# Two encoder layers on one core: one shift row on TensorE, sines in the opening, splits ahead of head roots, late rows in VectorE's gap, column sums asked for one unit on

## The chip, the cores and the metric

One core of one Trainium2 chip. The metric is the device time of one execution in microseconds (us), the median of three runs.

## What is computed

Two layers work on x of 1024 tokens by 1024 channels. Layer 0 has sliding-window attention with per-head sinks, query and key norms and rotary positions; layer 1 has a gated MLP whose gate is mixed along the sequence by a triangular 128x128 matrix per channel group. A squared-ReLU MLP of width 4096 follows each. Ahead of every sub-layer stands an RMS norm whose gain and shift come from the conditioning vector c.

```python
cond = jax.nn.silu(c)
for i in range(DEPTH):                                   # DEPTH = 2
    mod = (cond @ mod_w[i] + mod_b[i])[:, None, :]
    shift1, scale1, gate1, shift2, scale2, gate2 = jnp.split(mod, 6, axis=-1)
    h = rms_norm(x, norm1_gain[i]) * (1 + scale1) + shift1
    y = swa_sink_attention(...) if i == 0 else gmlp_spatial_gating(...)
    x = x + gate1 * y
    h = rms_norm(x, norm2_gain[i]) * (1 + scale2) + shift2
    x = x + gate2 * squared_relu_mlp(h, mlp_w1[i], mlp_w2[i])
```

## The kernel before

Activations lie transposed in SBUF: eight chunks of 128 channels by 1024 tokens. Every float32 product with a weight is made of three matmuls, since both sides are split into a high part (fp32r) and the rest: `w_hi` by `h_hi`, `w_hi` by `h_lo`, `w_lo` by `h_hi`. A **unit** is one output chunk of 128 channels: eight steps k over the input chunks, six 512-column matmuls each (L1463), 48 in all. Where only half of the tokens is done, it is 24. Units go in pairs over two weight slots. For each, SyncE loads `w_raw`, ScalarE writes `w_hi` (`split_hi`, L493), GpSimd or VectorE writes `w_lo` (`split_lo`, `first_low`), and TensorE waits in `ready` (L1452) for `lo_done` and for its PSUM tile to be emptied (`evac`). A hook is a piece of other TensorE work set behind a step k of a unit. The engines' orders are written out by hand and joined by semaphores.

The modulation `cond @ mod_w` is made on VectorE: it adds 128x1024 rows, scaled by an element of `cond`, into an accumulator (one instruction a row, eight rows a part), TensorE transposes the accumulator (`mod_columns`, L1550), and VectorE sums the columns and adds the bias (`first_part`, `mod_part`). Places that matter here:

- **The opening.** SyncE loads x, 16 rows `mod_first` (eight of scale1, then eight of shift1) and two weight blocks. VectorE works out the angles of the rotary positions, then adds the scale rows into `mod_acc` and those shift rows into `qa` that TensorE does not take as small matmuls (L1615, `ROWS_BY_TENSOR`, 3 rows). The squares of x go over `ss_done`, a root on ScalarE, `ss_mm`, a reciprocal and a spread copy on VectorE, and transposes (`spread_norm`, L1583) to PSUM. Then h is made chunk by chunk: `scaled` (VectorE), `h_hi` (ScalarE, L517), `low` (VectorE, L1095). `normed_pair` (L1478) multiplies as chunks come.
- **The queries.** Pair 0 is the keys and the first half of a query pair. Four steps j follow. For each, ScalarE empties PSUM and squares (`first_half`, L580), VectorE adds the squares (L1187), TensorE sums them by head (`head_squares`, a hook, L1564), ScalarE takes roots and spreads reciprocals (`head_roots`), TensorE transposes them (`head_spread`, L1571), and VectorE rotates (`turn`), norms, and adds modulation rows between (`mods`, L896).
- **The closing of attention** (`closing`): the output projection in two halves of the tokens. Behind it VectorE adds the residual, sums squares, splits weights (L954), makes h, and adds 16 **late rows** (L967) by the counts of `LATE_ROWS`: the rows of parts 4 and 5 of the modulation, which `mod_columns(4)` and `mod_columns(5)` transpose.
- **The opening of the MLP** (`opening_pair`, L1521): the first pair of up-units, first on the first token half, then on the second as its h comes. `mod_columns(5)` follows it (L1548).
- **The gated MLP** (L1385 to L1446): `bn_stats` over v, then `mod_part(11)`, the aggregate, a memset of the mixing tile `ws`, loads of `ws` and `bias` by ScalarE's queue, and `blend` (L1827), the mixing matmuls of TensorE, hooked at k = 4 of the second u-unit.

Of the kernel before, what the change touches and what calls it, by code (L numbers as in the profile page):

```python
# [14 lines left out]
P = 128  # L15
# [19 lines left out]
ROWS_BY_TENSOR = 3  # L35
# [30 lines left out]
LATE_ROWS = ((0, 0, 1, 2, 1, 2, 2), (0, 0, 1, 0, 1, 1, 2, 0, 3))  # L66
# [7 lines left out]
def build(nc, x_in, c_in, pos_in, weights, mod_w, cols, mats, ws_in, bias_in, q_dram, v_dram, out):  # L74
# [5 lines left out]
    with ctx:  # L80
# [96 lines left out]
        first_used, row_cols = sem("first_used"), sem("row_cols")  # L177
# [310 lines left out]
        def _(act):  # L488
# [64 lines left out]
            for k in range(KC):  # L553
                if k % 2 == 0:
                    act.wait_ge(x_ld[k // 2], 16)
                nc.scalar.activation(square_tile(k), x[:, k, :], ACT.Square).then_inc(sq_done, 1)
            act.wait_ge(const_in, 48)
            nc.scalar.activation(root[:, 0:1], eps, ACT.Sqrt)
            act.wait_ge(ss_done, KC)
            for half in range(2):  # L560
                nc.scalar.activation(tmp[0:1, 1, columns_of(half)], pp[0][0:1, columns_of(half)], ACT.Sqrt,
                                     bias=eps[0:1, :], scale=1.0 / D).then_inc(sd_done, 1)
            split_hi(0, 0)
# [16 lines left out]
            def first_half(j):  # L580
# [5 lines left out]
                split_hi(j + 1, 1)  # L586
                act.wait_ge(evac[1], j + 1)
# [13 lines left out]
            act.wait_ge(angle, 1)  # L601
            nc.scalar.activation(cos[:, :], cos[:, :], ACT.Sin).then_inc(trig, 1)
            nc.scalar.activation(sin[:, :], sin[:, :], ACT.Sin).then_inc(trig, 1)
# [3 lines left out]
            first_half(0)  # L607


            for j in range(4):  # L610
# [17 lines left out]
                if j < 3:  # L628
                    load_mod(4 * j + 6, 0)
                    load_mod(4 * j + 7, 1)  # L630
                    first_half(j + 1)
# [252 lines left out]
        def _(dve):  # L884
# [21 lines left out]
            def mod_part(part, tile=None):  # L906

                dve.wait_ge(mod_mm, part + 1)
                V.memset(mod_acc[:, :], 0.0).then_inc(acc_zero, 1)
                dve.wait_ge(acc_zero, part)  # L910
# [21 lines left out]
            def closing(pair0, n, gate, late=False, first=None):  # L932
# [88 lines left out]
                split_lo(KC - 1)  # L1021
                dve.wait_ge(bc_done, 2 * n + 2)
# [8 lines left out]
                if late:  # L1031
                    late_rows(LATE_ROWS[1][KC])
                    mod_part(5, pp[2])
# [68 lines left out]
            first_row(KC + ROWS_BY_TENSOR, KC)  # L1102
# [4 lines left out]
            first_row(KC + ROWS_BY_TENSOR + 1, KC + 1)  # L1107
            first_row(KC + ROWS_BY_TENSOR + 2, KC + 2)
            for half in range(2):
                dve.wait_ge(ss_mm, half + 1)  # L1110
                own(V.reciprocal(inv[:, 4 * half:4 * half + 4], pp[2][:, HALF * half:HALF * half + 4]))
                V.tensor_copy(mod_t[:, 0, columns_of(half)].rearrange("p (b m) -> p b m", m=P),
# [811 lines left out]
```

## Time and profile before

| | us |
|---|---|
| median of 3 runs | 2365.39 |
| lowest, highest | 2364.77, 2367.08 |
| the profiled execution, its own time | 2365.93 |
| its span | 2364.1 |
| TensorE busy / VectorE / ScalarE / GpSimd | 2301.6 / 1256.7 / 693.6 / 759.9 |

The profile is one execution. Its rows give a start in us from the start of the span, a duration, and in brackets how long the engine stood idle ahead of the row and what ended that. 1.83 us of that execution's time lie outside its span.

### The profile page before, as it was taken

What the parts mean: (1) busy time and instruction counts of PE and PEld (TensorE: products, weight loads), DVE (VectorE), ACT (ScalarE), POOL (GpSimd) and SP (SyncE); (2) the same over time, 40 slices, a digit from 0 to 9 for tenths busy, and PEclk for the clock granted to TensorE, in tenths of its full rate; (3) what the DMA queues carried; (4) which work ended last, traced back from release to release, by engine and by line L of the source; (5) the groups of instructions that cost most, each with busy time, mean ns of one, the idle gap of its engine ahead of it and who ended that gap; (6) DMA issues with size and microseconds to landing.
All of it is one profiled execution on the core that took longest, in us unless ns stands there. A gap on an engine that the chain in (4) does not pass through costs nothing.

```text
span 2364.1 us, 29197 instructions
## 1 busy us (share of the span) xinstructions
PE 2301.6 (97%) x10332; PEld 1837.8 (78%) x10332; DVE 1256.7 (53%) x1562; ACT 693.6 (29%) x940; POOL 759.9 (32%) x566
## 2 busy tenths in 40 slices
PE   7898998999999999999999999999999999999999
PEld 5786676888888888777887888877788888888887
DVE  6677678565565564564334431456655455555321
ACT  3325533232232232233222210223323223322220
POOL 0123420544544452311221212122154455355221
PEclk7999999999999999999999999999999999999999
DMA  6353332122112212223333221122111111111112
GB/s 253 98 160 97 144 144 80 54 81 94 60 69 89 71 62 98 89 89 107 123 121 137 80 79 51 65 80 89 54 49 51 54 53 44 44 62 44 54 45 89
DMA packets 82119, 201.33 MB, mean 85 GB/s; under 512 B 23809, under 2 KB 29825, under 8 KB 81538
## 3 DMA queue, kind: packets, MB, share of 16 engines
q1 hardware_dynamic: 63650, 139.70, 17.6%
q10 hardware_dynamic: 18400, 60.69, 7.2%
q8 instruction: 45, 0.74, 0.1%
q14 instruction: 24, 0.20, 0.0%
HBM read 182.54 MB, written 16.78 MB: 84 GB/s over the span
## 4 chain that ended last, share of the span: by engine, by line
PE 83%; issue 12%; POOL 2%; DVE 2%; ACT 1%; DMA 0%; DVEq 0%; POOLq 0%; ACTq 0%; SPq 0%
PE pp L1463 61%; PE pp L1768 20%; PE pp L1832 1%; POOL pr L428 1%; POOL w_lo L414 1%; PE pp L1806 1%; DVE mod_t L947 1%; DVE h_lo L982 0%; PE pp L1557 0%; DMA w_raw<-weights 0%; PE pp L1578 0%; DVE mod_acc L896 0%; ACT w_hi L493 0%; ACT tmp L526 0%; PE pp L1587 0%
## 5 line engine op out<-in xcount | busy, mean ns | idle before, releaser
L414 POOL TENSOR_TENSOR w_lo<-w_raw,w_hi 128x1024 fp32r<-128x1024 f32 x144 | 349.3, 2426 | 1301.3 <-ACT w_hi L493 1301.3
L1463 PE MATMUL pp<-h_hi,w_hi 128*128 128x512 f32 x1824 | 603.7, 402 | 22.3 <-DVE h_lo L982 6.9
L1463 PE MATMUL pp<-h_lo,w_hi 128*128 128x512 f32 x1824 | 595.4, 397 | 0.0
L1463 PE MATMUL pp<-h_hi,w_lo 128*128 128x512 f32 x1824 | 595.1, 397 | 0.0
L1463 PEld LDWEIGHTS pp<-h_hi,w_hi 128*128 128x128 f32 x1824 | 341.0, 189 | 112.4 <-DVE h_lo L982 15.0
L1463 PEld LDWEIGHTS pp<-h_hi,w_lo 128*128 128x128 f32 x1824 | 344.7, 189 | 83.4
L1463 PEld LDWEIGHTS pp<-h_lo,w_hi 128*128 128x128 f32 x1824 | 344.8, 189 | 81.8
L1330 DVE SCALAR_TENSOR_TENSOR x<-pp,mod,x 128x512 f32<-128x512 f32 x336 | 252.1, 750 | 242.1 <-PE pp L1768 242.1
L493 ACT ACTIVATE w_hi<-w_raw 128x1024 fp32r<-128x1024 f32 x170 | 179.7, 1057 | 634.9 <-PE pp L1463 511.8
L1768 PE MATMUL pp<-c_lo,w_hi 128*128 128x512 f32 x672 | 265.8, 396 | 0.0
L1768 PE MATMUL pp<-c_hi,w_hi 128*128 128x512 f32 x672 | 265.8, 396 | 0.0
L1768 PE MATMUL pp<-c_hi,w_lo 128*128 128x512 f32 x672 | 265.8, 396 | 0.0
L1463 PE MATMUL pp<-hid_hi,w_hi 128*128 128x512 f32 x512 | 182.7, 397 | 3.0 <-DVE hid_lo L1430 2.2
L1463 PE MATMUL pp<-hid_hi,w_lo 128*128 128x512 f32 x512 | 181.9, 395 | 0.0
L1463 PE MATMUL pp<-hid_lo,w_hi 128*128 128x512 f32 x512 | 181.9, 395 | 0.0
L455 POOL TENSOR_TENSOR w_lo<-s_w,w_hi 128x768 fp32r<-128x768 f32 x96 | 122.8, 1297 | 117.8 <-ACT w_hi L704 117.8
L1768 PEld LDWEIGHTS pp<-c_lo,w_hi 128*128 128x128 f32 x672 | 126.3, 188 | 30.6
L1768 PEld LDWEIGHTS pp<-c_hi,w_hi 128*128 128x128 f32 x672 | 126.3, 188 | 30.5
L1768 PEld LDWEIGHTS pp<-c_hi,w_lo 128*128 128x128 f32 x672 | 126.3, 188 | 30.4
L1278 DVE SCALAR_TENSOR_TENSOR c_f<-pp,tmp 128x512 f32<-128x512 f32 x72 | 47.5, 687 | 180.3 <-ACT tmp L711 180.3
L455 POOL TENSOR_TENSOR w_lo<-w_raw,w_hi 128x256 fp32r<-128x256 f32 x96 | 97.5, 1016 | 104.9 <-ACT w_hi L704 102.1
L704 ACT ACTIVATE w_hi<-s_w 128x768 fp32r<-128x768 f32 x96 | 60.8, 634 | 209.1 <-PE pp L1768 155.9
(182 smaller groups left out, 2284.4 us busy)
## 6 DMA issues: line engine op xcount, KB each, us to landing
w_raw<-weights SPq DMA_DIRECT2D x218, 512.0 KB, 3.5
mod_t<-mod_w ACTq DMA_DIRECT2D x64, 512.0 KB, 4.0
mod_first<-mod_w SPq DMA_DIRECT2D x16, 512.0 KB, 15.4
mod_late<-mod_w ACTq DMA_DIRECT2D x2, 4096.0 KB, 22.8
v_dram<-v_out ACTq DMA_DIRECT2D x16, 512.0 KB, 5.3
vf<-v_dram ACTq DMA_DIRECT2D x16, 512.0 KB, 3.3
x<-x_in SPq DMA_DIRECT2D x4, 1024.0 KB, 8.1
qf<-q_dram SPq DMA_DIRECT2D x32, 128.0 KB, 2.2
```

The costliest lines, as they stand in the source:

```text
L414: nc.gpsimd.tensor_tensor(out=w_lo[:, s, :, :], in0=w_raw[:, s, :, :], in1=w_hi[:, s, :, :].bitcast(f32), op=ALU.subtract).then_inc(lo_don ...
L428: nc.gpsimd.tensor_tensor(out=pr[:, b, :, 0:P], in0=pr[:, b, :, 0:P], in1=small[:, b, 3, :].unsqueeze(2).to_broadcast([P, 4, P]), op=ALU.m ...
L455: nc.gpsimd.tensor_tensor(out=down_target(w_lo, part), in0=down_source(part, q), in1=down_target(w_hi, part).bitcast(f32), op=ALU.subtract ...
L493: nc.scalar.activation(w_hi[:, s, :, :], w_raw[:, s, :, :], ACT.Copy).then_inc(hi_done, 1)
L704: nc.scalar.activation(down_target(w_hi, part), down_source(part, q), ACT.Copy).then_inc(d_hi, 1)
L947: V.tensor_tensor(out=sumsq[:, columns_of(half)], in0=sumsq[:, columns_of(half)], in1=tmp[:, s, columns_of(half)], op=ALU.add).then_inc(ss ...
L1278: V.scalar_tensor_tensor(out=out, in0=src[:, columns_of(half)], scalar=0.0, in1=tmp[:, s, columns_of(half)], op0=ALU.max, op1=ALU.mult).th ...
L1330: V.scalar_tensor_tensor(out=xn, in0=banks[BANK[t]], scalar=mod[:, 6 * layer + GATE2, 2 * q + m:2 * q + m + 1], in1=xn, op0=ALU.mult, op1= ...
L1463: last = T.matmul((pp[s] if tile is None else tile)[:, cs], w[:, s, k, :], r[:, k, cs], start=(k == 0 and w is w_hi and r is hi), stop=(k ...
L1768: last = T.matmul(banks[BANK[t]], w[:, slot, k, :], r[:, i, OPERAND[t], :], start=(t in FRESH and i == 0 and w is w_hi and r is c_hi), sto ...
L1806: last = T.transpose(pp[2][:, P * b:P * b + P], tmp[:, s, P * b:P * b + P], ident[:, :])
L1832: last = T.matmul(pp[2][:, P * b:P * b + P], vf[:, s, b, :], ws[:, bass.ds(i, 1), :].rearrange("p a t -> p (a t)"), start=True, stop=True)
```

## The change

In the opening, ScalarE makes the sines ahead of the first root, and writes the spread copies that VectorE wrote; TensorE makes the token sums ahead of `mod_columns(0)`, and takes one shift row where it took three; VectorE takes seven and is put in another order. In the queries, `first_half` is cut in `first_copy` (copy and `split_hi`) and `first_square`, and the first `first_copy` stands ahead of `head_roots(0)`; two rows of `mods` go behind the addition of squares of j = 0. In the closing, `mod_columns(4)` is hooked one unit later and the token sums two steps later; one late row goes from the end to u = 7, and the last two ahead of the second half's h. `mod_columns(5)` goes ahead of the second half of the opening pair, into another PSUM tile, with a wait on `mod_done` behind the pair. In the gated MLP `mod_part(11)` goes behind the first two `normalised`, without its memset, and the first blend is hooked at k = 7.

```diff
-ROWS_BY_TENSOR = 3
+ROWS_BY_TENSOR = 1
-LATE_ROWS = ((0, 0, 1, 2, 1, 2, 2), (0, 0, 1, 0, 1, 1, 2, 0, 3))
+LATE_ROWS = ((0, 0, 1, 2, 1, 2, 2), (0, 0, 1, 0, 1, 1, 2, 1, 2))
...
+            act.wait_ge(angle, 1)
+            nc.scalar.activation(cos[:, :], cos[:, :], ACT.Sin).then_inc(trig, 1)
+            nc.scalar.activation(sin[:, :], sin[:, :], ACT.Sin).then_inc(trig, 1)
             act.wait_ge(const_in, 48)
...
+            for half in range(2):
+                act.wait_ge(inv_done, half + 1)
+                nc.scalar.activation(mod_t[:, 0, columns_of(half)].rearrange("p (b m) -> p b m", m=P),
+                                     inv[:, 4 * half:4 * half + 4].unsqueeze(2).to_broadcast([P, 4, P]),
+                                     ACT.Copy).then_inc(rb_done, 1)
...
-            act.wait_ge(angle, 1)
-            nc.scalar.activation(cos[:, :], cos[:, :], ACT.Sin).then_inc(trig, 1)
-            nc.scalar.activation(sin[:, :], sin[:, :], ACT.Sin).then_inc(trig, 1)
+            first_copy(0)
             head_roots(0, KV)
             load_mod(2, 0)
             load_mod(3, 1)
-            first_half(0)
+            first_square(0)
...
-            def mod_part(part, tile=None):
+            def mod_part(part, tile=None, last=False):
...
                 split_lo(KC - 1)
+                if late:
+                    late_rows(LATE_ROWS[1][KC])
                 dve.wait_ge(bc_done, 2 * n + 2)
...
                 if late:
-                    late_rows(LATE_ROWS[1][KC])
-                    mod_part(5, pp[2])
+                    mod_part(5, pp[1])
...
             dve.wait_ge(q_bc, 1)
             V.tensor_tensor(out=oa[:, 0, :], in0=oa[:, 0, :], in1=pp[2][:, :], op=ALU.mult).then_inc(k_roped, 2)
-            mods(2)
...
                 V.tensor_tensor(out=tmp[:, 0, :], in0=tmp[:, 0, :], in1=tmp[:, 1, :], op=ALU.add).then_inc(q_sum, 1)
+                if j == 0:
+                    mods(2)
...
-                mod_part(10 + half)
+                if half == 0:
+                    mod_part(10)
...
             dve.wait_ge(v_sc, 1)
+            dve.wait_ge(mod_mm, PARTS)
             V.memset(ws[64:128, :, 0:64], 0.0).then_inc(wsz, 1)
...
-                with dve.Fori(0, 3) as i:
+                if kb == 0:
+                    normalised(1, 1, 1)
+                    mod_part(PARTS - 1, last=True)
+                    gated(0, 0, more=False)
+                    gated(0, 1)
+                with dve.Fori(0 if kb else 1, 3) as i:
...
-                    unit(pair0 + 3, 1, hi, lo, halves=(0,), hooks={5: columns})
+                    unit(pair0 + 3, 1, hi, lo, halves=(0,))
...
-                unit(pair0 + 4, 0, hi, lo, halves=(1,), hooks={4: lambda: token_squares(n, 0)})
+                hooks = {1: columns, 6: lambda: token_squares(n, 0)} if columns else {4: lambda: token_squares(n, 0)}
+                unit(pair0 + 4, 0, hi, lo, halves=(1,), hooks=hooks)
...
+                if n == 1:
+                    pe.wait_ge(evac[1], pair)
+                    mod_columns(5, mf_used, 2 * KC, tile=pp[1])
                 for k in range(KC + LAG):
...
-                if n == 1:
-                    mod_columns(5, mf_used, 2 * KC, tile=pp[2])
...
-            mod_columns(0, first_used, KC)
...
                 last.then_inc(ss_mm, 1)
+            mod_columns(0, first_used, KC)
...
                 opening_pair(pair0, 2 * layer + 1, (pp[3], pp[0]))
+                if layer == 0:
+                    pe.wait_ge(mod_done, 6)
...
-                unit(kb * KC + U_GU // 2, 1, h_hi, h_lo, hooks={4: lambda: blend(kb * KC, 0, kb, 0)})
+                unit(kb * KC + U_GU // 2, 1, h_hi, h_lo, hooks={4 if kb else 7: lambda: blend(kb * KC, 0, kb, 0)})
```

VectorE in the opening, behind the eight scale rows, before. `qa` takes the shift rows, `inv` and `mod_t` are the norm's reciprocals and their spread, the two `col_sum` are parts 1 and 0 of the modulation, and `shift_b` waits for TensorE's rows:

```order
18 L1069 TENSOR_SCALAR qa<-mod_first,cond 128x1024
19 L1076 TENSOR_REDUCE col_sum<-pp 128x8
20 L1079 TENSOR_TENSOR mod<-col_sum,colt 128x8
21 L1105 SCALAR_TENSOR_TENSOR amp<-mod,colt 128x8
22 L1071 SCALAR_TENSOR_TENSOR qa<-mod_first,cond,qa 128x1024 x2
23 L1111 RECIPROCAL inv<-pp 128x4
24 L1112 COPY mod_t<-inv 128x512
25 L1111 RECIPROCAL inv<-pp 128x4
26 L1112 COPY mod_t<-inv 128x512
27 L1071 SCALAR_TENSOR_TENSOR qa<-mod_first,cond,qa 128x1024
28 L1116 TENSOR_TENSOR shift_b<-pp,colt 128x8
29 L1071 SCALAR_TENSOR_TENSOR qa<-mod_first,cond,qa 128x1024
```

The same place after:

```order
18 L1080 TENSOR_SCALAR qa<-mod_first,cond 128x1024
19 L1082 SCALAR_TENSOR_TENSOR qa<-mod_first,cond,qa 128x1024
20 L1118 RECIPROCAL inv<-pp 128x4 x2
21 L1082 SCALAR_TENSOR_TENSOR qa<-mod_first,cond,qa 128x1024 x2
22 L1087 TENSOR_REDUCE col_sum<-pp 128x8
23 L1090 TENSOR_TENSOR mod<-col_sum,colt 128x8
24 L1123 SCALAR_TENSOR_TENSOR amp<-mod,colt 128x8
25 L1082 SCALAR_TENSOR_TENSOR qa<-mod_first,cond,qa 128x1024 x2
26 L1128 TENSOR_TENSOR shift_b<-pp,colt 128x8
27 L1082 SCALAR_TENSOR_TENSOR qa<-mod_first,cond,qa 128x1024
```

Seven shift rows stand where five stood, six of them ahead of `shift_b` where there were four, and the two copies are gone from VectorE.

ScalarE ahead of the queries' loop, before (`root` and `tmp<-inv` are the head roots of the keys, `qa<-pp` the first copy of the queries, `w_hi<-w_raw` behind it the split for the next slot):

```order
26 L602 ACT_TABLE_LOAD
27 L602 ACTIVATE cos<-cos 128x1024
28 L603 ACTIVATE sin<-sin 128x1024
29 L570 ACT_TABLE_LOAD
30 L570 ACTIVATE root<-pp,colt 128x16
31 L575 ACTIVATE tmp<-inv 128x8x64 x2
32 L499 DMA mod_t<-mod_w 128x1024 x2
33 L585 ACTIVATE qa<-pp 128x1024
34 L493 ACTIVATE w_hi<-w_raw 128x1024
35 L588 ACTIVATE tmp<-qa 128x1024
```

and after:

```order
30 L593 ACTIVATE qa<-pp 128x1024
31 L493 ACTIVATE w_hi<-w_raw 128x1024
32 L578 ACTIVATE root<-pp,colt 128x16
33 L583 ACTIVATE tmp<-inv 128x8x64 x2
34 L499 DMA mod_t<-mod_w 128x1024 x2
35 L598 ACTIVATE tmp<-qa 128x1024
```

The split now waits for nothing but its weights and the end of pair 0; the sines and both table loads are gone from here.

## Rows read from the trace of the kernel before

**Rows 1.** The page, part 1: busy time, share of the span, instructions

```profile
PE 2301.6 (97%) x10332; PEld 1837.8 (78%) x10332; DVE 1256.7 (53%) x1562; ACT 693.6 (29%) x940; POOL 759.9 (32%) x566
```

**Rows 2.** TensorE's waits: who waited for whom, us in total, times, longest

```profile
PE pp L1557 <- DVE mod_acc L896: 2.5, 1, 2.5
```

**Rows 3.** The timeline of TensorE in the opening: start, us, instruction, idle before it

```profile
33.98 10.40 PE L1615 MATMUL pp<-cond,mod_first 128*128 128x1 f32 x48
...
52.57 1.19 PE L1463 MATMUL pp<-h_hi,w_hi 128*128 128x512 f32 x2 [4.64 <-DVE h_lo L1095]
```

**Rows 4.** The timeline of VectorE in the opening

```profile
18.90 9.63 DVE L1071 SCALAR_TENSOR_TENSOR mod_acc<-mod_first,cond,mod_acc 128x1024 f32<-128x1024 f32 x7
30.87 0.75 DVE L1069 TENSOR_SCALAR qa<-mod_first,cond 128x1024 f32<-128x1024 f32 x1 [2.34 <-DMA mod_first<-mod_w]
...
44.42 0.17 DVE L1116 TENSOR_TENSOR shift_b<-pp,colt 128x8 f32<-128x8 f32 x1 [6.26 <-PE pp L1615]
...
49.40 0.17 DVE L1079 TENSOR_TENSOR mod<-col_sum,shift_b 128x8 f32<-128x8 f32 x1
```

**Rows 5.** The timeline of TensorE in the queries

```profile
96.21 1.22 PE L1463 MATMUL pp<-h_hi,w_hi 128*128 128x512 f32 x2 [3.37 <-POOL w_lo L414]
...
100.55 1.04 PE L1571 MATMUL pp<-ident,tmp 128*128 128x128 f32 x8
...
108.65 2.72 PE L1564 MATMUL pp<-colt,tmp 128*128 128x4 f32 x16 [2.87 <-DVE tmp L1187]
111.23 1.20 PE L1463 MATMUL pp<-h_hi,w_hi 128*128 128x512 f32 x2
...
122.07 1.03 PE L1571 MATMUL pp<-ident,tmp 128*128 128x128 f32 x8
...
137.82 1.84 PE L1564 MATMUL pp<-colt,tmp 128*128 128x4 f32 x16
139.52 0.71 PE L1463 MATMUL pp<-h_hi,w_hi 128*128 128x512 f32 x2
...
147.99 1.04 PE L1571 MATMUL pp<-ident,tmp 128*128 128x128 f32 x8
```

**Rows 6.** The timeline of ScalarE in the queries

```profile
119.43 1.02 ACT L585 ACTIVATE qa<-pp 128x1024 f32<-128x1024 f32 x1 [5.58 <-DVE mod_acc L896]
```

**Rows 7.** The timeline of VectorE in the queries

```profile
102.86 4.60 DVE L896 SCALAR_TENSOR_TENSOR mod_acc<-mod_t,cond,mod_acc 128x1024 f32<-128x1024 f32 x2
...
108.52 1.27 DVE L1182 SCALAR_TENSOR_TENSOR oa<-qa,qgain,cos 128x1024 f32<-128x1024 f32 x1
...
116.36 2.66 DVE L896 SCALAR_TENSOR_TENSOR mod_acc<-mod_t,cond,mod_acc 128x1024 f32<-128x1024 f32 x2
```

**Rows 8.** The timeline of TensorE in the closing of attention

```profile
325.72 1.05 PE L1578 MATMUL pp<-ones,mod_t 128*128 128x1 f32 x8 [0.73 <-DVE mod_t L947]
```

**Rows 9.** The timelines at the MLP's opening: VectorE, then GpSimd, then TensorE

```profile
377.89 1.41 DVE L974 SCALAR_TENSOR_TENSOR tmp<-x,amp,pp 128x512 f32<-128x512 f32 x2 [2.89 <-PE pp L1587]
...
396.03 2.64 POOL L414 TENSOR_TENSOR w_lo<-w_raw,w_hi 128x1024 fp32r<-128x1024 f32 x1 [70.92 <-ACT w_hi L493]
...
401.74 1.19 PE L1463 MATMUL pp<-h_hi,w_hi 128*128 128x512 f32 x2 [4.12 <-DVE tmp L1278]
...
406.81 0.62 PE L1463 MATMUL pp<-h_hi,w_hi 128*128 128x512 f32 x2
```

**Rows 10.** The timelines at the first blend: VectorE, then TensorE

```profile
1282.37 0.91 DVE L909 MEMSET mod_acc<- 128x1024 f32 x1 [3.53 <-PE pp L1557]
...
1294.20 2.05 PE L1832 MATMUL pp<-ws,vf 128*128 128x128 f32 x8 [2.31 <-issue]
...
1297.53 0.72 PE L1463 MATMUL pp<-h_hi,w_hi 128*128 128x512 f32 x2
```

**Rows 11.** Windows of TensorE: stretch, length, busy, granted clock, DMA share, GB/s

```profile
319.00:320.00 1.00, 1.00 (x9) 1.00 0.00 0
...
402.00:404.00 2.00, 2.00 (x5) 0.50 0.61 240
```

More of the change, by code:

```diff
@@ L176, in build @@
         pos_s, pos_f, pos_b = sem("pos_s"), sem("pos_f"), sem("pos_b")
-        first_used, row_cols = sem("first_used"), sem("row_cols")
+        first_used, row_cols, inv_done = sem("first_used"), sem("row_cols"), sem("inv_done")
         dv = sem("dv")
@@ L578, in head_roots, with first_copy @@
                 ins.then_inc(q_rb, 1)
-            def first_half(j):
+            def first_copy(j):
                 act.wait_ge(gemm, U_Q + 2 * j + 1)
@@ L586, in first_half, with first_square @@
                 split_hi(j + 1, 1)
+            def first_square(j):
                 act.wait_ge(evac[1], j + 1)
@@ L630, in _ @@
                     load_mod(4 * j + 7, 1)
-                    first_half(j + 1)
+                    first_copy(j + 1)
+                    first_square(j + 1)
             nc.scalar.activation(root[:, 0:1], root[:, 0:1], ACT.Exp)
@@ L904, in mod_step @@
                 scale_add(mod_t[:, slot, :], k, mt_used)
-            def mod_part(part, tile=None):
+            def mod_part(part, tile=None, last=False):
                 dve.wait_ge(mod_mm, part + 1)
-                V.memset(mod_acc[:, :], 0.0).then_inc(acc_zero, 1)
-                dve.wait_ge(acc_zero, part)
+                if not last:
+                    V.memset(mod_acc[:, :], 0.0).then_inc(acc_zero, 1)
+                    dve.wait_ge(acc_zero, part)
                 V.tensor_reduce(out=col_sum[:, :], in_=(pp[3] if tile is None else tile)[:, :].rearrange("p (k c) -> p k c", c=P),
@@ L1101, in _ @@
                 first_row(q, q)
-            first_row(KC + ROWS_BY_TENSOR, KC)
+            rows = [KC + ROWS_BY_TENSOR + i for i in range(KC - ROWS_BY_TENSOR)]
+            first_row(rows[0], KC)
+            first_row(rows[1], KC + 1)
+            for half in range(2):
+                dve.wait_ge(ss_mm, half + 1)
+                V.reciprocal(inv[:, 4 * half:4 * half + 4], pp[2][:, HALF * half:HALF * half + 4]).then_inc(inv_done, 1)
+            first_row(rows[2], KC + 2)
+            first_row(rows[3], KC + 3)
             first_part(1, SCALE1, mod_b(SCALE1))
@@ L1106, in _ @@
                                        op0=ALU.add, op1=ALU.mult))
[L1107 to L1112, printed above, removed]
-                              inv[:, 4 * half:4 * half + 4].unsqueeze(2).to_broadcast([P, 4, P])).then_inc(rb_done, 1)
-            first_row(KC + ROWS_BY_TENSOR + 3, KC + 3)
+            first_row(rows[4], KC + 4)
+            first_row(rows[5], KC + 5)
             dve.wait_ge(row_cols, 1)
             own(V.tensor_tensor(out=shift_b[:, :], in0=pp[1][:, 0:KC], in1=mod_b(SHIFT1), op=ALU.add))
-            first_row(KC + ROWS_BY_TENSOR + 4, KC + 4)
-            first_low(0)
+            first_row(rows[6], KC + 6)
             dve.wait_ge(bc_done, 2)
             scaled(0, 0)
+            scaled(1, 1)
             first_part(2, SHIFT1, shift_b[:, :])
-            scaled(1, 1)
+            first_low(0)
             dve.wait_ge(mod_done, 2)
```

## The prediction

> **What bounds the kernel now.** I read the page's first part before anything else: TensorE is busy for 2301.6 us of 2364.1 [rows 1], so only its idle 62.5 us, and what it does at its lower clock, can be won. The next view is its waits, longest first, and then the timelines around each. Six places matter: the start of the first unit at 52.57 [rows 3], two waits in the queries of 3.37 and 2.87 us [rows 5], 2.5 us for late rows [rows 2], 0.73 us behind it [rows 8], 4.12 us at the opening of the MLP [rows 9] and 2.31 us at the first blend [rows 10]. The change touches all of them and little else.
>
> A wait costs twice where the granted clock falls with it: in windows it reads 0.50, which is 1.2 GHz, or 1.00, which is 2.4 GHz [rows 11]. At full speed the 18 groups of two 512-column matmuls from 139.52 to 147.99 take 8.47 us, 0.47 each; the same 18 from 111.23 to 122.07 take 10.84 [rows 5]. So the clock lost 2.4 us there. After 2.5 us of idle at the late rows the clock still read 1.00 in the window 319:320 [rows 2, 11]; after 2.87 it had fallen.
>
> **The change, part by part.** Times below are of the profiled execution: span 2364.1, its own time 2365.93, 0.5 above the median 2365.39. I subtract from all alike.
>
> *The opening.* TensorE's first unit starts when h of chunk 0 is there, which hangs on part 0 of the modulation, made at 49.40+0.17 = 49.57 [rows 4]. VectorE's chain to it holds 2.34 us idle for a row's DMA and 6.26 idle for TensorE's three rows [rows 4]. These are 48 matmul records in 10.40 us [rows 3], so one row is 16 records, 3.5 us, and its wait goes: TensorE gets to it about when the reciprocals are made. New chain, from the end of the scale rows at 28.53 (18.90+9.63): row 9 at once (0.75); row 10 when it has landed. Row 11 landed at 30.87 and rows come at about 1.27 us (412 GB/s in this stretch, half a MB each, an estimate of mine), so row 10 ends near 30.9; reciprocals 0.4; rows 11 and 12, 2.6; sum, bias and gain of part 1, 1.65; rows 13, 14, 15, 3.8; `shift_b` 0.2; two `scaled` 2.4; reduction and bias 1.4. That ends at 43.4, 6.2 us earlier than 49.57. The moved `first_low` (1.2) lies under ScalarE's `h_hi`. The sines, 2.1 us and a table load, fall in 6.6 us in which ScalarE waited for the sum of squares; were that cover gone, they would cost their 3.4. The spread copies on ScalarE are hidden behind rows 11 and 12. What follows the first chunk is the same chain at the same clock, so the gain stays: **6.2**, from 5 (rows landing later than I reckon) to 7.
>
> *The queries.* `w_lo` for slot 1 of pair 1 came late since its split stood behind the head roots. With `first_copy(0)` ahead it starts when pair 0 ends, some 11 us earlier than before, and TensorE needs it 8 us after it is there. The 3.37 go, and the six groups from 96.21 to 100.55 take 2.8 instead of 4.34 [rows 5]: 4.9 together. Then the 2.87 us for the sum of squares. Its way was VectorE's two `mods`, 4.60 us [rows 7], which now stand behind it; it needs ScalarE's square, which follows the transposes by 2.1 us, and one addition of 1.2, while TensorE has three steps (4.2 us) to do. So it is there 1 us early. 2.87 go, the sums take 1.7 (137.82 to 139.52) and not 2.58, and 2.4 come back from the 18 groups [rows 5]: 6.2. Together 11.1.
>
> What is late next: VectorE's rows came only some 4.8 us earlier, TensorE 11. In times of before less the gain of the opening: `mods` end at 103.7, the turn takes 7.84 (108.52 to 116.36), the copy on ScalarE follows the next `mods` by 3.07 after their start (119.43) [rows 6, 7], so at 114.6; split 0.9 later, GpSimd 1.1 after that, and 2.4 to 3.4 for `w_lo`: 119.1 to 120.1. TensorE wants it at 118.8 (122.07+7.8-11.1). I take a wait of **0.5**, from 0 to 3.3 us, and count 2.4 more for the clock at the upper end. Net **10.6**, from 5.4 to 11.1.
> These rows of `mods` took 4.60 us for two where 2.66 is the rule [rows 7], with GpSimd's split running over them. The Trainium skill (SBUF — State Buffer, Who interferes with whom) says that a VectorE instruction with two SBUF inputs and a GpSimd instruction that reads SBUF shut each other out whole, and that whoever issues first has the port. By that rule, with `mods` first, they would end 1.9 us earlier and the wait would be nil: 10.6 would be 11.1.
>
> *The closing.* `mod_columns(4)` waited 2.5 us for the accumulator [rows 2]. Four half-steps later, 0.7 us each, it finds it done; the token sums, two steps later, lose their 0.73 [rows 8]. The spread norm keeps its place; its copy on VectorE is ready 0.8 us before TensorE gets there by my count. **3.2**, from 2.4.
>
> *The MLP's opening.* Before, `mod_columns(5)`, `mod_part(5)` and then the first quad stood between the pair and the next unit: 4.12 us idle. Two late rows now lie in a gap of 2.89 us [rows 9], 2.66 of it by the pace of [rows 7], one more in a gap ahead of the reciprocal. The transposes run while TensorE waits for h anyway. VectorE is then free for the quad about 5 us earlier, and the last to come is GpSimd's `w_lo`, 396.03+2.64 = 398.67 [rows 9]. TensorE starts at 398.7 instead of 401.74: 3.0. Its idle time falls to some 2 us, less than the 2.5 that left the clock up; I take it as kept, and then six groups (401.74 to 406.81) take 2.8 and not 5.07. **5.3**, or 3.0 with the clock lost. The new wait on `mod_done` ends at about 395.1, before the pair does; behind it only TensorE's next unit is queued.
> The Trainium skill (TensorE: Matmul & The Clock Gate, What's actually happening) says that the monitor of the clock runs freely, so where it falls differs from run to run. The trace agrees: 2.31 us at the blend lost the clock and 2.5 at the late rows did not. By that rule 5.3 and 3.0 are both open.
>
> *The gated MLP.* VectorE stood idle 3.53 us for `mod_columns(11)` [rows 10] with the aggregate and the memset of `ws` behind it. Now the aggregate runs at once, and only the memset waits. Loads of `ws` and `bias` come some 4 us earlier, and the blend is asked for three steps (4.2 us) later: its 2.31 us go. It takes 3.33 us at half clock (1294.20 to 1297.53) [rows 10], some 1.7 at full: **3.9**, from 2.3. The later blend leaves VectorE 1.7 us less room than a unit to finish chunk 0 ahead of the next blend, by my count enough.
>
> Sum: 6.2 + 10.6 + 3.2 + 5.3 + 3.9 = **29.2 us**. Span 2334.9, this execution's time 2336.7, median 2365.39 - 29.2 = **2336.2**.
>
> **The rivals.**
> - *The split chain becomes the bound in the queries.* `w_lo` for unit (2,1) is late by 3.3 us and the clock falls. For it: VectorE gained less than TensorE there. Against: no step after it has changed. It gives 5.2 us less, 2341.4.
> - *The clock falls at the MLP's opening.* 2.3 us less, 2338.5. For it: 2.31 us at the blend were enough. Against: the idle is shorter.
> - *The opening is bound by DMA.* If rows 9 and 10 land late and the chain follows the last row (35.9) anyway, its gain is 5 and not 6.2. If in place of this TensorE's own row were late, `shift_b` would wait again as before (6.26), and the change would not do there what it says: 2342.5.
> - *Slower.* One mechanism only could do that: TensorE stays at 1.2 GHz after its opening. It is idle or lightly loaded from about 33 to 46 us as before, then starts earlier. Each us of full-speed matmul time costs up to 0.8 more at half clock (0.85 against 0.47 us a group), so the gain of 29.2 is gone after 36 us of such work, and the whole stretch to 187 us, 141 us, would give 114 more and so about 2450. Against: at every wait of before the clock was back within 6 us [rows 5, 9].
>
> **How the numbers follow.** The forecast has 0.58 (2334 to 2338.5 within its own bounds), the clock at the MLP 0.17, the split chain 0.13, the opening short 0.08, slower 0.01; 0.03 for a gain of less than 4.7 us by reasons that I don't see. The range takes all bounded cases: gains of 21 to 33, 2332 to 2344. A change of 0.2%, 4.7 us, is about what a measurement of this kernel can tell from none. Faster 0.96, same 0.02, slower 0.02.
>
> **What would show it.** The first unit starts at 46.4, with VectorE idle under 1 us between 31 and 43. No wait for `w_lo` in pair 1, none for the sum of squares, at most 1 us at unit (2,1). No wait at `mod_columns(4)`. At the MLP's opening TensorE's wait is for GpSimd's `w_lo`, 2 us, and granted clock 1.00 behind it. No wait at the blends. What would make it wrong: a new wait of over 3 us on TensorE anywhere, above all at the splits of the queries or the second blend, or a start later than 48 us.

## The result: 29 us less, a ratio of 0.988

The changed kernel takes 2337.28 us, the median of four runs (2335.88 to 2337.90), beside 2366.23 for the kernel before in the same comparison (2364.77 to 2367.61). The ratio is 0.9877, with a 95% interval from 0.9860 to 0.9894. The profiled execution took 2337.90 us with a span of 2336.1, 28.0 less than the span before. The forecast was 2336.2 with a range of 2332 to 2344.

The page of the changed kernel, part 1, answers to [rows 1]:

```profile
PE 2283.9 (98%) x10300; PEld 1822.4 (78%) x10300; DVE 1255.2 (54%) x1561; ACT 694.0 (30%) x941; POOL 760.5 (33%) x566
```

TensorE has 32 matmul records fewer, those of the two shift rows, and 17.7 us less busy time. So of the 28.0 us, 17.7 are work that now runs at full clock or not at all, and 10.3 are idle time.

TensorE's waits in the changed kernel (who waited for whom, us in total, times, longest) answer to [rows 2]; the 2.5 us for late rows that stood there are not in the list any more:

```profile
PE pp L1579 <- DVE qa L1082: 5.7, 1, 5.7
...
PE pp L1483 <- POOL w_lo L414: 4.6, 3, 1.7
PE pp L1673 <- DVE pp L1176: 2.9, 1, 2.9
PE pp L1483 <- DVE hid_lo L1445: 2.2, 1, 2.2
```

In the opening, the timeline of TensorE and then that of VectorE answer to [rows 3] and [rows 4]:

```profile
29.43 2.16 PE L1637 MATMUL pp<-cond,mod_first 128*128 128x1 f32 x16
...
39.33 1.97 PE L1579 MATMUL pp<-ident,qa 128*128 128x128 f32 x8 [5.73 <-DVE qa L1082]
45.99 1.19 PE L1483 MATMUL pp<-h_hi,w_hi 128*128 128x512 f32 x2 [4.70 <-DVE h_lo L1106]
```

```profile
28.56 0.76 DVE L1080 TENSOR_SCALAR qa<-mod_first,cond 128x1024 f32<-128x1024 f32 x1
29.55 1.28 DVE L1082 SCALAR_TENSOR_TENSOR qa<-mod_first,cond,qa 128x1024 f32<-128x1024 f32 x1 [0.23 <-DMA mod_first<-mod_w]
...
37.78 0.16 DVE L1128 TENSOR_TENSOR shift_b<-pp,colt 128x8 f32<-128x8 f32 x1
...
42.83 0.17 DVE L1090 TENSOR_TENSOR mod<-col_sum,shift_b 128x8 f32<-128x8 f32 x1
```

`shift_b` waits for nothing now and the one row on TensorE takes 2.16 us. VectorE is idle 0.23 us between row 9 and row 10, where it was idle 2.34 and then 6.26. The part is made at 43.00 instead of 49.57 and the first unit starts 6.58 us earlier.

In the queries, the timeline of TensorE answers to [rows 5]:

```profile
88.89 1.04 PE L1593 MATMUL pp<-ident,tmp 128*128 128x128 f32 x8
...
113.30 0.73 PE L1483 MATMUL pp<-h_hi,w_hi 128*128 128x512 f32 x2 [1.14 <-POOL w_lo L414]
```

Both waits of before are gone, and one of 1.14 us for `w_lo` stands at the unit that the prediction named. The granted clock behind it is 1.00 in the windows up to 214 us.

At the closing of attention, at the MLP's opening and at the first blend, TensorE's timeline answers to [rows 8], [rows 9] and [rows 10]:

```profile
303.93 1.03 PE L1579 MATMUL pp<-ident,mod_acc 128*128 128x128 f32 x8
...
308.29 0.95 PE L1600 MATMUL pp<-ones,mod_t 128*128 128x1 f32 x8
...
378.67 0.73 PE L1483 MATMUL pp<-h_hi,w_hi 128*128 128x512 f32 x2 [1.71 <-POOL w_lo L414]
...
1270.40 1.95 PE L1856 MATMUL pp<-ws,vf 128*128 128x128 f32 x16
```

Of four waits (2.50, 0.73, 4.12 and 2.31 us) one is left, 1.71, and it is now for GpSimd. The row of the blend in [rows 10] holds eight of its sixteen matmuls; all sixteen took 3.58 us there, mostly at half clock, against 1.95 here. The windows of TensorE behind the wait of 1.71 us (stretch, length, busy, granted clock, DMA share, GB/s) answer to the half clock of [rows 11]:

```profile
378.00:380.00 2.00, 1.33 (x6) 1.00 0.56 213
380.00:390.00 10.00, 10.00 (x45) 1.00 0.44 153
```

To see where the time came from, I set the start of the same TensorE instruction in both kernels side by side, at a place behind each stage. The lead is the difference of the two:

| behind | lead, us | this step | forecast |
|---|---|---|---|
| opening (first unit) | 6.58 | 6.58 | 6.2 |
| queries (last head sums) | 16.53 | 9.95 | 10.6 |
| attention (first to last P·V) | 15.20 | -1.34 | 0 |
| closing (second spread norm) | 18.94 | 3.74 | 3.2 |
| MLP's opening (first down product) | 25.24 | 6.30 | 5.3 |
| v part, first blend (second blend) | 29.65 | 4.41 | 3.9 |
| output units of the gated MLP, end | 28.08 | -1.57 | 0 |

Five steps came out near their terms; two stages that the change does not touch gave back 2.9 us. The experiments are on both.

### The profile page after: what moved, and what is told of

Its sections match the earlier page's. It is cut to its first block, busy times and chain, and to the rows that moved or that the text cites. A ratio compares the mean times of both kernels' runs of the same rounds, so it can differ in the third digit from the quotient of the medians.

```text
span 2336.1 us, 29125 instructions
## 1 busy us (share of the span) xinstructions
PE 2283.9 (98%) x10300; PEld 1822.4 (78%) x10300; DVE 1255.2 (54%) x1561; ACT 694.0 (30%) x941; POOL 760.5 (33%) x566
## 4 chain that ended last, share of the span: by engine, by line
PE 87%; issue 10%; DVE 1%; ACT 1%; POOL 1%; DMA 0%; DVEq 0%; POOLq 0%; ACTq 0%
PE pp L1483 63%; PE pp L1790 20%; PE pp L1856 1%; POOL w_lo L414 1%; PE pp L1830 1%; PE pp L1710 1%; PE pp L1699 1%; PE pp L1673 1%; ACT pr L662 1%; PE pp L1579 0%; PE pp L1600 0%; DVE mod_t L957 0%; DVE small L1245 0%; DVE h_lo L992 0%; ACT h_hi L675 0%
```

## The experiments

All times below are single executions unless a median is named. The kernel before took 2367.29 us beside the first four and 2366.99 beside the next four, one run each; beside the last four it had a median of 2367.11 in seven runs, from 2364.86 to 2369.93. Whole times of one execution therefore cannot part differences of two or three us. Each stage is read by the lead of TensorE as in the table above, which also keeps it apart from what later stages do.

**The opening: three rows again in the new order.**

```diff
-ROWS_BY_TENSOR = 1
+ROWS_BY_TENSOR = 3
@@ VectorE
-            first_row(rows[5], KC + 5)
-            first_row(rows[6], KC + 6)
```

> The changed kernel with three shift rows on TensorE again, five on VectorE, all else as changed. Theory A (the prediction's words: TensorE's row products were the long wait, 10.40 us for three, and one row ends it): the three take 10.4 us again, the transposes follow at about 42, VectorE's scaled waits for them, and the first unit starts near 48.5 in place of 45.99; time some 2.5 us longer. Theory B (the length came from the lower clock, to which TensorE had fallen in its 3.00 us wait for mod_acc; with the token sums ahead it stays at full clock): the 48 records take about 6.5 us, from 29.4 to 36, nothing waits for them, and the first unit starts at 46.0 within 0.3, as with one row.

It took 2339.13 us, and the first unit started at 49.01, 3.0 us later than in the changed kernel. The timelines of TensorE and then of VectorE in this kernel:

```profile
28.66 1.59 PE L1577 MATMUL pp<-ident,mod_acc 128*128 128x128 f32 x8 [1.40 <-DVE mod_acc L1082]
30.05 10.24 PE L1635 MATMUL pp<-cond,mod_first 128*128 128x1 f32 x48
```

```profile
40.32 0.17 DVE L1127 TENSOR_TENSOR shift_b<-pp,colt 128x8 f32<-128x8 f32 x1 [1.32 <-PE pp L1635]
42.20 2.47 DVE L1100 SCALAR_TENSOR_TENSOR tmp<-x,amp,pp 128x1024 f32<-128x1024 f32 x2 [1.71 <-PE pp L1607]
```

The granted clock was 0.78 from 28 to 30 us and 0.50 behind that, so the 48 records took 10.24 us. `shift_b` and the transposes of the spread are late for VectorE, 1.32 and 1.71 us, where the changed kernel waits for neither. With three rows TensorE's products are on the chain, with one they are not; two rows were not tried.

**The other side: the kernel before with one row.**

```diff
-ROWS_BY_TENSOR = 3
+ROWS_BY_TENSOR = 1
@@ VectorE, before shift_b and behind it
+            first_row(KC + ROWS_BY_TENSOR + 4, KC + 4)
+            first_row(KC + ROWS_BY_TENSOR + 5, KC + 5)
...
-            first_row(KC + ROWS_BY_TENSOR + 4, KC + 4)
+            first_row(KC + ROWS_BY_TENSOR + 6, KC + 6)
```

> The kernel before with one shift row on TensorE and seven on VectorE (three more of them ahead of shift_b), nothing else changed. Theory A (the count of rows is the gain of the opening): first unit near 46.5. Theory B (count and order share it): the 16 records take 3.5 us at half clock, VectorE makes six rows and two copies ahead of shift_b, and the first unit starts at 48.3 by my count, so 4.3 us of the 6.6 earlier than 52.57. The rest of the profile as before, time 4 to 5 us under the kernel before.

It took 2363.99 us. The first unit started at 47.79, a lead of 4.78 of the 6.58. So the number of rows alone is worth 4.8 us, and as the last step on top of all others it is worth the 3.0 of the experiment above; the rest of the opening (the order of VectorE, ScalarE's copies and sines, the earlier token sums) is worth 1.8 or 3.6, and its pieces were not undone one by one. The parts overlap, so the 6.58 have no fixed shares. Behind the queries only 2.41 us of the lead were left. The waits of TensorE there are those of before, to 0.01 us:

```profile
PE pp L1465 <- POOL w_lo L414: 5.1, 2, 3.4
...
PE pp L1566 <- DVE tmp L1189: 2.9, 1, 2.9
```

Its windows behind the second of them:

```profile
104.00:106.00 2.00, 0.90 (x5) 0.53 0.95 383
106.00:108.00 2.00, 2.00 (x11) 0.50 0.93 365
108.00:112.00 4.00, 4.00 (x12) 0.50 0.01 3
112.00:116.00 4.00, 4.00 (x14) 0.70 0.16 23
```

The clock is at half for some ten us there, where in the kernel before the same wait was followed by some seven. The lead was 4.8 us before and behind the wait of 3.37, and 3.55 before and behind the one of 2.87; it fell to 3.55 and then to 2.4 in the half-clock stretches behind them. So the waits themselves took nothing of the lead; TensorE stayed at half clock longer behind both. Whether the earlier start brought that about or it differs between executions, this one profile does not show.

**The queries: the first copy back behind the head roots.**

```diff
-            first_copy(0)
             head_roots(0, KV)
             load_mod(2, 0)
             load_mod(3, 1)
+            first_copy(0)
             first_square(0)
```

> The changed kernel with head_roots(0) and its two loads ahead of first_copy(0) again; the sines stay in the opening. Theory A (the order of the copy and split against the head roots made the wait for w_lo of 3.37): the copy is at 84.1, the split at 85.1, GpSimd ends at 88.6 to 89.5, TensorE wants it at 86.1, so it waits 2.5 to 3.4 us for w_lo and loses 0 to 1.6 to the clock; time 2.5 to 4.9 longer than changed, less up to 1.1 where the later wait at unit (2,1) shrinks by it. Theory B (the sines and their two table loads made it late): no wait, same time.

It took 2340.57 us; the lead behind the queries was 12.77 instead of 16.53. TensorE's timeline has the wait of [rows 5] back to the hundredth:

```profile
89.58 0.72 PE L1483 MATMUL pp<-h_hi,w_hi 128*128 128x512 f32 x2 [3.37 <-POOL w_lo L414]
```

Its windows behind the wait:

```profile
90.00:92.00 2.00, 2.00 (x10) 1.00 0.74 184
92.00:94.00 2.00, 2.00 (x14) 1.00 0.19 78
```

The clock stayed at 1.00, so the wait cost 3.6 us and no more, though it is the longest of the queries; the other 0.2 is the next wait for `w_lo`, 1.33 us instead of 1.14. Behind the same 3.37 us in the kernel before, the clock had fallen: it was 0.50 from 96 to 98 us.

**The queries: VectorE's two modulation rows back ahead of the sum of squares.**

```diff
             V.tensor_tensor(out=oa[:, 0, :], in0=oa[:, 0, :], in1=pp[2][:, :], op=ALU.mult).then_inc(k_roped, 2)
+            mods(2)
...
-                if j == 0:
-                    mods(2)
```

> The changed kernel with the two rows of mods behind k_roped again, ahead of the addition of squares. Theory A (those rows made the wait of 2.87 at the token sums): VectorE ends them at 91.2+4.7 = 95.9, adds to 97.1, TensorE wants the sum at 93.9 and so waits 3.2 us; the clock falls, 3.3 us more; the wait of 1.14 at unit (2,1) goes. Time 4.5 to 5.5 us longer than changed, or 2 if the clock stays. Theory B (the earlier split alone, with VectorE no longer slowed by GpSimd, would have cured it): wait under 0.5 us, same time.

It took 2340.68 us; the lead behind the queries was 11.70. The wait for the sum is back, and this time the clock fell. TensorE's timeline, then its windows:

```profile
96.94 2.75 PE L1585 MATMUL pp<-colt,tmp 128*128 128x4 f32 x16 [2.87 <-DVE tmp L1199]
```

```profile
97.00:99.00 2.00, 2.00 (x14) 0.72 0.93 365
99.00:101.00 2.00, 2.00 (x8) 0.50 0.39 158
```

So each of the two moves in the queries removes the wait that it was made for, 3.37 and 2.87 us. Undone singly they cost 3.8 and 4.8, of which the second pays some 3 in clock and saves the 1.14 at the next unit, since `w_lo` is then in time for a TensorE that comes later.

**The sines back at their old place.**

```diff
-            act.wait_ge(angle, 1)
-            nc.scalar.activation(cos[:, :], cos[:, :], ACT.Sin).then_inc(trig, 1)
-            nc.scalar.activation(sin[:, :], sin[:, :], ACT.Sin).then_inc(trig, 1)
             act.wait_ge(const_in, 48)
...
+            act.wait_ge(angle, 1)
+            nc.scalar.activation(cos[:, :], cos[:, :], ACT.Sin).then_inc(trig, 1)
+            nc.scalar.activation(sin[:, :], sin[:, :], ACT.Sin).then_inc(trig, 1)
             first_copy(0)
```

> The changed kernel with the two sines back in the queries, directly ahead of first_copy(0), and with it two table loads. Theory A (the move of the sines is worth nothing by itself; what counts is the order of copy and head roots): sines end at about 74.1 (70.7+1.3+2.1), the copy follows 1 us later than changed, w_lo is ready at 79, TensorE wants it at 86; the roots' table load fits ahead of 80.6. Same time within 0.5 us of the trace's points. Theory B (it takes part in the gain): a wait of over 1 us in pair 1.

It took 2337.50 us, and the lead behind the queries was 16.46. Once the copy stands ahead of the roots, the sines' place shows no gain beyond 0.1 us: this path has slack enough ahead of TensorE.

**The closing: the column sums of part 4 asked for one unit earlier again.**

```diff
-                    unit(pair0 + 3, 1, hi, lo, halves=(0,))
+                    unit(pair0 + 3, 1, hi, lo, halves=(0,), hooks={5: columns})
...
-                hooks = {1: columns, 6: lambda: token_squares(n, 0)} if columns else {4: lambda: token_squares(n, 0)}
+                hooks = {4: lambda: token_squares(n, 0)}
```

> The changed kernel with mod_columns(4) at k = 5 of the last unit of the first half and the token sums at k = 4, as before. Theory A (the hook's place is the whole gain of the closing, and none of it is owed to a shift of VectorE): waits of 2.5 us there and 0.7 at the token sums come back, at full clock; time 3.2 to 3.8 us longer. Theory B (VectorE, which got ahead elsewhere, would have been in time): under 1 us.

It took 2343.04 us. The step of the closing was -1.61 us instead of +3.74. TensorE's timeline and windows:

```profile
305.08 1.92 PE L1579 MATMUL pp<-ident,mod_acc 128*128 128x128 f32 x8 [2.50 <-DVE mod_acc L905]
```

```profile
304.00:306.00 2.00, 0.92 (x5) 0.79 0.46 186
306.00:308.00 2.00, 2.00 (x8) 0.50 0.03 8
308.00:310.00 2.00, 2.00 (x9) 0.85 0.00 0
```

The wait came back at the very 2.50 us of [rows 2], and 0.75 for the token sums with it. Undoing the step cost 5.35 in all, 1.6 more than the 3.74 it had gained, since here the clock fell behind the wait. In the kernel before the same wait left it at 1.00 [rows 11].

**The MLP's opening: late rows, column sums and their place back.**

```diff
-LATE_ROWS = (..., (0, 0, 1, 0, 1, 1, 2, 1, 2))
+LATE_ROWS = (..., (0, 0, 1, 0, 1, 1, 2, 0, 3))
@@ VectorE: the late rows of step KC and mod_part(5, pp[2]) again behind the last low()
@@ TensorE
-                    mod_columns(5, mf_used, 2 * KC, tile=pp[1])
                 for k in range(KC + LAG):
...
+                    mod_columns(5, mf_used, 2 * KC, tile=pp[2])
-                if layer == 0:
-                    pe.wait_ge(mod_done, 6)
```

> The changed kernel with the late rows, mod_columns(5) and its tile as before, and without the wait on mod_done. Theory A: TensorE's wait of 4.1 us behind the opening pair comes back and with it six groups at half clock, so 6.3 us longer (4.1 and 2.2), by the forecast 5.3. Of that 0.8 us the forecast did not have: h of the second half ran 1.68 us a chunk in the changed kernel where it ran 1.68 and 1.92 in turn; if that comes from the filled gap, the pace of before is back here; if it is chance, it stays as in the changed kernel and the loss is 5.5.

It took 2343.05 us; the step was 0.42 us instead of 6.30. TensorE's timeline, then its windows:

```profile
382.28 1.19 PE L1482 MATMUL pp<-h_hi,w_hi 128*128 128x512 f32 x2 [4.12 <-DVE tmp L1290]
```

```profile
382.00:384.00 2.00, 1.72 (x4) 0.50 0.60 176
384.00:388.00 4.00, 4.00 (x11) 0.50 0.36 125
```

The wait of 4.12 us of [rows 9] and the half clock behind it are back: 5.88 of the 6.30 us hang on this part, whose three pieces (late rows, place of the column sums, place of their addition) were undone together only. The 0.42 left are in the pair itself, where VectorE delivers a chunk of the second half's h each 1.68 us. In the kernel before, every second of the first steps took 1.9. The even pace stayed in this kernel, so it does not come from the filled gap; what makes it is open.

**The gated MLP: each of its two edits undone, and both.** The first puts the eleventh column sums back ahead of the statistics, with their memset:

```diff
-                if half == 0:
-                    mod_part(10)
+                mod_part(10 + half)
...
-            dve.wait_ge(mod_mm, PARTS)
...
-                    mod_part(PARTS - 1, last=True)
```

> The changed kernel with mod_part(11) ahead of the aggregate again, with its memset; the blend stays at k = 7. Theory A (the later hook alone covers the loads): the loads land at about 1269, 4 us later than changed, TensorE asks at 1270.4, no wait, same time. Theory B (VectorE's order was the gain): a wait of 0.5 us or more ahead of the blend, or at the second blend, where VectorE has less room.

The second puts the blend back at the fourth block:

```diff
-hooks={4 if kb else 7: lambda: blend(kb * KC, 0, kb, 0)})
+hooks={4: lambda: blend(kb * KC, 0, kb, 0)})
```

> The changed kernel with the first blend of the gated MLP asked for after the fourth block of its unit again, as before the change, instead of the seventh; the eleventh column sums stay in VectorE's new place. Theory A (the new order of VectorE covers the wait by itself): in the changed kernel the blend's weights and bias are asked for at 1260.3 to 1262.4 us and have landed by 1264.9, and TensorE would ask at about 1266.2 (1270.4 less three blocks of 1.40): no wait at the blend, the granted clock stays 1.00, the span is that of the changed kernel, 2336.1 (2335 to 2337.5). Rival B (the later place on TensorE is what covers it): a wait of 1 to 2.3 us at the blend with the clock at half behind it, a span 2.5 to 4 us longer, 2338.6 to 2340.

The third has both diffs:

> The changed kernel with both edits of the gated MLP's opening undone: the eleventh column sums ahead of the statistics with their memset, and the blend asked for after the fourth block. Theory A: the wait of 2.31 us is back at the blend and the clock falls behind it, as before the change: TensorE's lead over the kernel before grows by 0 there instead of 4.1 to 4.4, so the span is 2340.0 to 2340.6. Rival B (the lead came from another part of the change, since either edit alone keeps it): no wait, 2336 to 2338.

They took 2339.52, 2333.97 and 2343.60 us; the step from the first down product to the second blend was 4.44, 4.43 and 0.28 us, beside 4.41 in the changed kernel. Only with both undone does TensorE wait. The timeline of TensorE without both edits, its windows, and then the timeline with the blend alone moved back:

```profile
1270.26 2.56 PE L1853 MATMUL pp<-ws,vf 128*128 128x128 f32 x16 [2.33 <-issue]
```

```profile
1270.00:1272.00 2.00, 1.74 (x14) 0.89 0.00 0
1272.00:1274.00 2.00, 2.00 (x8) 0.50 0.59 166
1274.00:1276.00 2.00, 2.00 (x8) 0.75 0.24 96
```

```profile
1263.81 1.95 PE L1856 MATMUL pp<-ws,vf 128*128 128x128 f32 x16
```

Either edit covers the wait of 2.3 us, and the pair of them is worth 4.1: the wait, and 1.8 for the clock. The prediction had taken them as one. The whole times of these three differ by more than that, and most of the rest lies in attention, where they ran at -2.99, +0.97 and -2.86 us. The 3.3 us by which the second kernel beats the changed one do not come from the blend: its step there is the same, and it is ahead by 2.3 us at the end of attention already, where the two kernels have not differed yet. The next experiment is on that.

**The changed kernel once more.** No edit.

> The changed kernel as it is, profiled once more. Theory A (whether TensorE's clock falls behind a wait of 2 to 3 us, and for how long, is not set by the kernel's order but varies between executions): the waits are the same within 0.1 us (2.94 at the sinks, 2.16 ahead of the gated MLP's output units), but the lead over the kernel before that is lost at one of the two differs from that of the first profile (1.34 and 1.55 us) by 0.5 us or more. Rival B (the kernel's order sets it): both within 0.1 us of the first profile, a span of 2336.1 within 0.3.

It took 2337.68 us, and the lead behind every stage was within 0.3 us of that in the first profile: in attention it lost 1.07 us and at the gated MLP's output units 1.58, beside 1.34 and 1.57. Of this pair rival B is the nearer one, without its 0.1 us. But with the blend moved, a kernel that is word for word the same until 1264 us gained 0.97 us in attention and lost nothing at the output units. The windows of TensorE at the sinks, in the changed kernel:

```profile
214.00:216.00 2.00, 0.00 (x0) 0.78 0.00 0
216.00:218.00 2.00, 1.90 (x12) 0.50 0.04 8
```

The windows of the kernel with the blend moved back alone, and the row of its wait:

```profile
214.00:216.00 2.00, 0.27 (x4) 1.00 0.00 0
216.00:218.00 2.00, 1.62 (x16) 1.00 0.14 46
```

```profile
215.73 0.71 PE L1673 MATMUL pp<-kf,qf 64*128 64x128 f32 x8 [2.94 <-DVE pp L1176]
```

The wait is 2.94 us in both. The clock fell with it in one execution and not in the other, and that is worth 2.3 us; at 1550 us the same holds for a wait of 2.16 and 1.6 us. Over all fourteen profiles the step of attention lay between -2.99 and +0.97 us against the kernel before. Two waits are in it. At the sinks TensorE waits 2.9 us in each profile, and the clock fell in all but two, the one with the blend moved back and the one with VectorE's rows moved back; in the kernel before it fell too (0.52 from 234 to 236 us), which is why a step above zero is possible. And near 190 us TensorE waits 1.3 to 1.7 us for the DMA of the queries; the clock fell there in six profiles, for about 1.2 to 1.5 us each, and in the changed kernel in neither.

Five of the profiles are of kernels that are the same, step for step, up to 1260 us: the changed one twice, and those with either or both edits of the gated MLP undone. Their steps of attention were -1.34, -1.07, -2.99, +0.97 and -2.86. So in attention the order of the kernel's steps does not settle it. The loss at the output units was 1.5 to 1.6 us in seven profiles and nothing in the other seven, the kernel before among them; there no two executions of one kernel differed, so an effect of the order is not excluded. What settles it is open: it may be chance, or the instant at which the wait falls, and the profiles do not part these.

**One step further: the copy ahead of the loads in the later pairs too.**

```diff
                 if j < 3:
+                    first_copy(j + 1)
                     load_mod(4 * j + 6, 0)
                     load_mod(4 * j + 7, 1)
-                    first_copy(j + 1)
                     first_square(j + 1)
```

> The changed kernel with one more step: in each later pair of query units too, ScalarE copies the product out of PSUM and writes the high half of the next weights before it issues the two loads of modulation weights, which wait for VectorE (at 106.20 us in the profile of the changed kernel, and the copy follows at 107.97). Theory A: the high half is then written from about 103.4 to 104.4 instead of 108.9 to 109.9, GpSimd's low half by about 107.9 instead of 113.3, and the wait of 1.14 us of the unit at 113.30 is gone; nothing else is late in its place, since the loads start at 106.2 as before. 1.1 us less than the changed kernel, up to 1.6 with the clock: a median of 2336.1 beside 2337.3, ratio 0.9872. Rival B (the loads, behind the copy, the split and the square on ScalarE, come later and VectorE's modulation products with them): a wait for the column sums at the next unit of roots, and 0 to 2 us more than the changed kernel.

The median of four runs was 2336.44 us (2336.27 to 2337.75), a ratio of 0.9873 to the kernel before, from 0.9856 to 0.9889. GpSimd's timeline:

```profile
104.32 2.91 POOL L414 TENSOR_TENSOR w_lo<-w_raw,w_hi 128x1024 fp32r<-128x1024 f32 x1 [9.66 <-ACT w_hi L493]
```

In the changed kernel that split started at 110.02. The wait of 1.14 us is gone and the lead behind the queries is 17.94, 1.41 more than in the changed kernel. In this profile attention gave back 2.62 us instead of 1.34, and the difference is not from the sinks but from the earlier wait for the queries' DMA. TensorE's row there, and its window behind it:

```profile
190.46 0.75 PE L1673 MATMUL pp<-kf,qf 64*128 64x128 f32 x8 [1.67 <-DMA qf<-q_dram]
```

```profile
191.00:193.00 2.00, 2.00 (x12) 0.50 0.77 214
```

In the changed kernel the same wait was 1.70 us and the clock stayed at 1.00. The two medians are 0.8 us apart and the runs overlap, so a gain in the whole time is not shown; that the wait is gone is.

## Why the prediction was right, and where its terms were off

The total came out within 1.1 us of the forecast by medians, and that is in part luck. By the lead, the five terms together gave 31.0 us where the sum had 29.2, and two stages that the sum left out took back 2.9.

*The opening* was 6.58 against 6.2. The chain ran as it was added up, 43.00 instead of 43.4, and VectorE's idle time in it was 0.23 us for a row's DMA where I had allowed for more. The two experiments on the number of rows support the step that carries it: TensorE's products are on the chain with three rows and off it with one. The cover named for the sines was there too. ScalarE's timeline:

```profile
18.79 1.06 ACT L558 ACTIVATE cos<-cos 128x1024 f32<-128x1024 f32 x1
19.75 1.04 ACT L559 ACTIVATE sin<-sin 128x1024 f32<-128x1024 f32 x1
...
25.44 1.25 ACT L564 ACTIVATE tmp<-pp,colt 1x512 f32<-1x512 f32 x2 [3.13 <-PE pp L1621]
```

Behind both sines and their tables ScalarE still waits 3.13 us for the sum of squares.

*The queries* were 9.95 against 10.6. The two waits went, each by its own move. The new wait for `w_lo` was at the unit named, 1.14 us where 0.5 was taken from a range of 0 to 3.3. `mods` took 4.79 us for two behind the sum, as slow as before [rows 7]. The prediction had them end 1.9 us earlier if they came first; GpSimd's split started at 92.05 and `mods` at 92.33, so they did not. ScalarE's copy came only once its loads had been let go by VectorE, at 107.97.

*The attention* was left out of the sum, as a stage that nothing touches, and lost 1.34. This is what the working had wrong: at a wait of 2.9 us which the change leaves alone the clock can still come out differently, worth up to 2.3 us, and the range was to hold this for all the waits left, not only for the one at the MLP. The same goes for the 1.57 at the end.

*The closing* was 3.74 against 3.2, with no wait at the column sums and none at the token sums. Undoing it cost 5.35, 1.6 more than it had gained, by the clock. In the prediction I had used the 1.00 of the window behind that wait [rows 11] to say that 2.5 us leave the clock up; one run with the very same wait read 0.50. So that reason was worth less than it looked.

*The MLP's opening* was 6.30 against 5.3. TensorE's wait is 1.71 us for GpSimd's `w_lo`, as named, and the clock stayed up. Most of the surplus is GpSimd's start: 376.25 with a lead of 18.94 stands against 396.03 before, 0.84 us sooner, since the pair ahead of it ended sooner. VectorE's even pace is a part of that.

*The first blend* was 4.1 to 4.4 against 3.9. The mechanism held, but it is there twice: either edit does it, so of the two edits one was not needed for this wait.

*The rivals.* The split chain came as a wait of 1.14 us and not as the bound; the clock did not fall at the MLP; the opening was neither bound by DMA nor by TensorE's row. The slower case did not show: the first unit ran at half clock for its first five us, and from 52 to 214 us the granted clock was 1.00. One reason given against it was wrong all the same: the clock was not back within 6 us at every wait of before. Behind the wait that ended at 108.65 it was still 0.64 from 115 to 117 us.

## What to carry to other kernels

Put a wait's price at its length plus the clock, and the clock's part at a range from nothing to 3 us, for the waits that are left in the kernel, touched or not. Here that holds for those over 2 us, and for waits of 1.5 to 1.7 us in attention, where TensorE has much idle time; the waits of 1.7 us for `w_lo` between full units kept the clock in every profile that has them. When an early stage is sped up, follow the lead behind each later wait: here one row instead of three alone gave 4.8 us at the start and kept 2.4 behind the queries, lost at half clock and not by longer waits. Where two edits aim at one wait, forecast each alone too, since one may be enough. And compare stages by the lead of one instruction, since the whole time of a single execution holds every fall of the clock in it.

## What the runs showed of the hardware

The granted clock did not follow the length of a wait. It stayed at 1.00 behind 3.37 us of idle TensorE (the kernel with the copy behind the roots) and at 2.94 (the one with the blend moved back and the one with VectorE's rows moved back), and fell to 0.50 at 2.16, 2.33, 2.50, 2.87 and 2.94 in others, and in six profiles at 1.5 to 1.7 (the wait for the queries' DMA). The same wait in the same place went either way: 3.37 us for `w_lo`, 2.50 at the late rows, 2.94 at the sinks, 2.16 at the output units.

The Trainium skill (TensorE: Matmul & The Clock Gate, What's actually happening) says that the monitor runs freely and does not restart with the kernel, so that the point at which the clock changes varies; it says so of the rise at a kernel's start. These pairs are in line with it for the fall, without showing that this is the cause.

One fall cost 1.6 us at the output units and 1.6 at the late rows (5.35 less 3.74; the kernel before had the same waits and no fall), 1.8 at the first blend, 2.3 at the sinks and some 3 behind the sum of squares. In two profiles (the copy behind the roots, and the late rows moved back) the clock also fell near 1070 us, where no wait is over 1 us but three of 0.32, 0.96 and 0.70 us follow each other, and that cost 0.5 us; in the other profiles it stayed at 1.00 there.

A row of 16 one-column products with its weight loads took 2.16 us in the changed kernel, where the granted clock was still 1.00 until 30 us, and 3.4 each in the kernel with three rows, at 0.50. I had taken 3.5 as the price of a row whatever its place.
